# Top-2 expert routing rewritten: raw rows gathered, norms applied afterwards, choice per 128 tokens, overflow test moved into the first expert

## The reference

```
x = x + recurrent_mixer(rms_norm(x, norm_mix[1]), ...)
h = rms_norm(x, norm_ffn[1])
logits = h @ w_router                     # 8 experts
top_logits, top_idx = lax.top_k(logits, 2)
gates = softmax(top_logits)
# rows of h sorted by expert, in blocks of 128
y = (silu(xb @ w_gate[e]) * (xb @ w_up[e])) @ w_down[e]
x = x + sum over the token's two experts of gate * y
```

## Time and profile before

| | us |
|---|---|
| median of 3 runs | 2413.49 (2413.48 to 2413.81) |
| the profiled execution | 2411.67 |
| its span, first to last instruction | 2409.9 |
| PE busy | 2354.2 (98%) |
| DVE busy | 1801.3 (75%) |
| ACT busy | 1439.8 (60%) |
| chain that ended last | PE 88%, DVE 7%, ACT 2% |

### The profile page before, as it was taken

How to read it: one execution, slowest core, us unless ns; L and a number is a source line. 1 busy time by engine, 2 the same in 40 slices (tenths; PEclk the granted TensorE clock), 3 DMA queues, 4 the chain that set the end, 5 groups by cost and what they waited for, 6 DMA issues and landing times.

```text
span 2409.9 us, 30511 instructions
## 1 busy us (share of the span) xinstructions
PE 2354.2 (98%) x12200; PEld 1961.4 (81%) x12200; DVE 1801.3 (75%) x2391; ACT 1439.8 (60%) x1993; POOL 6.6 (0%) x15
## 2 busy tenths in 40 slices
PE   8999999799999999999999998999999999999998
PEld 7888888688888888888888886779988877898887
DVE  6755558798989898989898987676755577757554
ACT  5444446577777777777777775455444454545443
POOL 0000000000000000000000000000000000000000
PEclk9999999999999999999999999999999999999999
...
GB/s 277 122 192 184 184 181 161 186 343 361 349 357 359 366 338 357 358 371 345 351 358 360 360 334 165 168 121 179 171 189 182 175 187 122 140 176 167 194 185 58
DMA packets 277764, 586.40 MB, mean 243 GB/s; under 512 B 9216, under 2 KB 61568, under 8 KB 277616
## 3 DMA queue, kind: packets, MB, share of 16 engines
...
...
## 4 chain that ended last, share of the span: by engine, by line
PE 88%; DVE 7%; ACT 2%; issue 1%; DMA 0%; SPq 0%; DVEq 0%; ACTq 0%
PE ps L106 85%; PE ps L109 4%; DVE low_wlo L121 4%; ACT low_whi L115 1%; DMA low_raw<-in_hy_w_in 0%; ACT L112 0%; DVE low_nv L127 0%; ACT s_p L112 0%; ACT low_junk L112 0%; DVE s_rot L121 0%; DVE s_sm L121 0%; DVE s_G L121 0%; ACT rg_ra L112 0%; ACT s_zu L112 0%; DVE low_x L121 0%
## 5 line engine op out<-in xcount | busy, mean ns | idle before, releaser
L121 DVE TENSOR_TENSOR low_wlo<-low_raw,low_whi 128x1024 fp32r<-128x1024 f32 (+1 forms) x990 | 1159.3, 1214 | 364.0 <-ACT low_whi L115 362.9
L115 ACT CAST low_whi<-low_raw 128x1024 fp32r<-128x1024 f32 (+1 forms) x990 | 983.7, 1043 | 457.0 <-PE ps L106 444.4
L106 PE MATMUL ps<-low_whi,low_hTh 128*128 128x512 f32 (+2 forms) x1360 | 535.4, 394 | 7.3 <-DVE low_wlo L121 5.7
L106 PE MATMUL ps<-low_whi,low_hTl 128*128 128x512 f32 (+2 forms) x1360 | 521.3, 383 | 0.0
L106 PE MATMUL ps<-low_wlo,low_hTh 128*128 128x512 f32 (+2 forms) x1360 | 520.5, 383 | 0.0
L106 PEld LDWEIGHTS ps<-low_whi,low_hTh 128*128 128x128 f32 x1360 | 257.6, 189 | 55.1 <-DVE low_hTl L127 3.8
L106 PEld LDWEIGHTS ps<-low_whi,low_hTl 128*128 128x128 f32 x1360 | 256.9, 189 | 51.0
L106 PEld LDWEIGHTS ps<-low_wlo,low_hTh 128*128 128x128 f32 x1360 | 257.8, 190 | 44.5 <-issue 0.5
L106 PE MATMUL ps<-low_whi,ffn_Th 128*128 128x512 f32 x608 | 246.5, 405 | 0.0
L106 PE MATMUL ps<-low_wlo,ffn_Th 128*128 128x512 f32 x608 | 240.7, 396 | 0.0
L106 PE MATMUL ps<-low_whi,ffn_Tl 128*128 128x512 f32 x608 | 198.0, 396 | 0.0
...
## 6 DMA issues: line engine op xcount, KB each, us to landing
...
```

The costliest lines, as they stand in the source:

```text
L106: return self.real.matmul(*a, **k) if self.real else WALK
L115: return self.real.copy(*a) if self.real else WALK
L121: return self.real.tensor_tensor(*a) if self.real else WALK
```

## The change

1. The rows gathered are those of raw x: `hh` and `hl` are made from x, and `hf`, `grow` and its load go. The gain of the norm is applied to the gathered rows: `act_gather` and `dve_gather` work in two pieces of 128x256 with a scale per partition, for all pairs. The root is applied later: `pe_er` multiplies the one-hots with the root (one column per expert), `er` then scales the gate product in the silu and the up product in `f_h`. `pe_er` for experts 0 and 1 stands in step 0 before gate k-tile 5, for the other six in step 4 before up k-tile 5.
2. Choice, ranks, places and one-hots are made for each half of the tokens: `dve_choose`, `pe_ranks`, `dve_places`. The one-hots of half 0 are multiplied with the first 128 columns of a bank before those of half 1 exist (`pe_gather_first`).
3. The root is made once for both halves (`dve_rstd`), at the end of `dve_route`.
4. The shares are made in steps 2 to 4; the exp stands on ACT at the start of step 3. The table of silu is loaded at the end of `act_route`.
5. `where_over` stands before step 6 on PE, ACT and DVE, and on SP before the first load that waits for a unit after e0.u6.0. The piece that it skips uses other banks and other memory.
6. On ACT the cast of e0.g0.1 comes before `hh` of half 1, that of e0.u0.0 after the gather.

The diff, cut to its core (the removed lines stand above):

```diff
                     pe_router_x(e, 0, 0)
                 if (tb, n_half, n, q) == (1, 0, 1, 0):
                     pe_router_x(e, 0, 1)
+                if (tb, n_half, n, q) == (1, 0, 1, 1):
                     pe_router(e, 0, 0)
                 if (tb, n_half, n, q) == (1, 1, 0, 2):
                     pe_router(e, 0, 1)
...
+                t = e.matmul(AB[tb][:, 0:8], hT32[:, q, tb * 128:tb * 128 + 128], rw[:, q, :], start=q == 0, stop=q == 7)
+            if n:
+                t.then_inc(*mark("sum", "logits", tb))
...
+        def pe_gather_first(e, q, tb):
...
+            e.wait_ge(*at("hot", 1, tb))
+            e.wait_ge(*at("hl", tb, q // 2))
+            for i, t_ in ((0, 0),) if tb == 0 else ((0, 1), (1, 0), (1, 1)):
+                s, o = slice(128 * (2 * q + i), 128 * (2 * q + i) + 128), b[:, 256 * i:256 * i + 256]
+                e.matmul(o, hh[:, t_, s], S1[:, t_, 0:256], start=t_ == 0, stop=False)
+                t = e.matmul(o, hl[:, t_, s], S1[:, t_, 0:256], start=False, stop=t_ == 1)
+            if tb:
+                t.then_inc(*mark("gathered", 0, q))
...
+            for f in (2 * q, 2 * q + 1):
+                t = e.activation(xgs[p % 2][0][:, f, :], turns["gather", p, q][:, 256 * (f % 2):256 * (f % 2) + 256],
+                                 AF.Identity, scale=k("norm", 24 + f, 1))
+            t.then_inc(*mark("xh", p, q))
...
+            for f in (2 * q, 2 * q + 1):
+                t = e.scalar_tensor_tensor(xl[:, f, :], turns["gather", p, q][:, 256 * (f % 2):256 * (f % 2) + 256],
+                                           k("norm", 24 + f, 1), xh[:, f, :].bitcast(F32), MUL, SUB)
+            t.then_inc(*mark("xl", p, q))
...
+        def pe_er(e, x0, x1):
+            e.wait_ge(*at("rstd", "all"))
+            e.wait_ge(*at("hot", x1 - 1, 1))
+            for x_ in range(x0, x1):
+                for tb in range(2):
+                    t = e.matmul(b[:, x_:x_ + 1], S1[:, tb, 128 * x_:128 * x_ + 128].bitcast(F32), rs[:, 1, tb, 0:1],
+                                 start=tb == 0, stop=tb == 1)
+            t.then_inc(*mark("sum", "er", x0))
...
+        def pe_ranks(e, tb):
+            P = open_bank(e, 4, ("ranks", tb))
+            e.wait_ge(*at("chosen", tb))
+            t = e.matmul(P[:, 0:8], strict[:, :], Mb[:, tb, :], start=True, stop=tb == 0)
...
+            t.then_inc(*mark("sum", "ranks", tb))
         def pe_route(e):
             pe_router_x(e, 1, 0)
             pe_router_x(e, 1, 1)
+            pe_ranks(e, 0)
             pe_router(e, 1, 0)
+            pe_gather_first(e, 0, 0)
             pe_router(e, 1, 1)
...
+            for q in range(1, 4):
+                pe_gather_first(e, q, 0)
+            pe_ranks(e, 1)
             for q in range(4):
-                pe_gather(e, 0, q)
+                pe_gather_first(e, q, 1)
...
         def act_route(e):
+            for n in range(2):
+                act_hh(e, 0, n)
+                act_hT32(e, 0, n)
             act_sq(e, 3, 0, 0)
-            act_hT32(e, 0, 0)
             act_sq(e, 3, 0, 1)
-            act_hT32(e, 0, 1)
-            act_sq(e, 3, 1, 0)
-            act_hh(e, 0, 0)
-            act_hh(e, 0, 1)
+            hi_after(e, "rg.o.2")
+            act_hh(e, 1, 0)
             act_hT32(e, 1, 0)
             act_hT32(e, 1, 1)
+            act_hh(e, 1, 1)
+            act_sq(e, 3, 1, 0)
             act_sq(e, 3, 1, 1)
-            hi_after(e, "rg.o.2")
-            hi_after(e, "rg.o.3")
-            act_hh(e, 1, 0)
-            act_hh(e, 1, 1)
-            e.wait_ge(*at("share", 0))
-            e.activation(mexp, mdiff, AF.Exp).then_inc(*mark("share_e", "all"))
             for q in range(4):
                 act_gather(e, 0, q)
+            hi_after(e, "rg.o.3")
+            e.activation(msm[:, 254:255], msm[:, 255:256], AF.Silu)
...
+        def dve_rstd(e):
+            v, w, u = (nv[:, :, y] for y in range(3))
             for tb in range(2):
+                for n in range(2):
+                    e.wait_ge(*at("sq", 3, tb, n))
+            e.scalar_tensor_tensor(v, ss[:, :, 0], D * EPS, ss[:, :, 1], ADD, ADD).then_inc(*mark("step"))
+            rsqrt(e, v, w, u, False)
+            e.tensor_scalar(rs[:, 1, :, 0], w, -1 / 256, None, MUL).then_inc(*mark("rstd", "all"))
...
+        def dve_choose(e, tb):
+            e.wait_ge(*at("sum", "logits", tb))
...
+            e.tensor_tensor(meq[:, tb], mL[:, tb, :].unsqueeze(1).to_broadcast([128, 2, 8]),
+                            mtop[:, tb, 0:2].unsqueeze(2).to_broadcast([128, 2, 8]), EQ).then_inc(*mark("step"))
+            e.tensor_scalar(mnth[:, tb:tb + 1], mtop[:, tb, 0:1], mtop[:, tb, 1:2], 1.0, EQ, ADD).then_inc(*mark("step"))
+            e.wait_ge(sg.sem("step"), sg.count["step"] - 1)
+            e.tensor_tensor_scan(mcs[:, tb].rearrange("p k e -> p (k e)"), d0[:, :, :].rearrange("p k e -> p (k e)"),
+                                 meq[:, tb].rearrange("p k e -> p (k e)"), 0.0, MUL, ADD).then_inc(*mark("step"))
+            e.wait_ge(*now("step"))
...
+            e.tensor_tensor(Mb[:, tb, :], mmask[:, tb, 0], mmask[:, tb, 1], ADD).then_inc(*mark("chosen", tb))
...
+        def dve_places(e, tb):
+            n = 16 if tb else 8
+            e.wait_ge(*at("sum", "ranks", tb))
+            e.tensor_copy(posc[:, 8 * tb:8 * tb + n], AB[0][:, 0:n]).then_inc(*mark("ranks", tb))
+            e.wait_ge(*now("step"))
+            dve_hot(e, 0, tb)
+            dve_hot(e, 1, tb)
...
         def dve_route(e):
             dve_residual(e, 3, 0, 0)
             dve_residual(e, 3, 0, 1)
...
+            dve_hl(e, 0, 0)
+            dve_hl(e, 0, 1)
+            dve_choose(e, 0)
             dve_residual(e, 3, 1, 0)
...
             dve_residual(e, 3, 1, 1)
...
+            dve_places(e, 0)
+            dve_hl(e, 1, 0)
+            dve_choose(e, 1)
+            dve_hl(e, 1, 1)
+            dve_places(e, 1)
+            lo_after(e, "rg.o.2", 0)
+            dve_gather(e, 0, 0)
+            dve_gather(e, 0, 1)
+            lo_after(e, "rg.o.2")
+            dve_gather(e, 0, 2)
+            dve_gather(e, 0, 3)
+            lo_after(e, "rg.o.3")
+            dve_rstd(e)
+        def dve_share(e):
+            e.tensor_reduce(mmax, posc[:, 16:24], AX.X, MAX).then_inc(*mark("step"))
+            e.tensor_tensor(mdiff, mtop[:, :, 1], mtop[:, :, 0], SUB).then_inc(*mark("step"))
+            e.wait_ge(*at("rstd", "all"))
             e.wait_ge(*now("step"))
...
+            e.tensor_tensor(mdiff, rs[:, 1, :, 0], mdiff, MUL).then_inc(*mark("share", 0))
             e.tensor_copy(cnt[:, :], mmax).then_inc(*mark("count", "all"))
...
+        def act_share(e):
+            e.wait_ge(*at("share", 0))
+            e.activation(mexp, mdiff, AF.Exp).then_inc(*mark("share_e", "all"))
...
-            where_over(e, pe_overflow)
             for c_, (x_, f) in enumerate(STEPS):
+                if c_ == 6:
+                    where_over(e, pe_overflow)
                 for q in pe_gate_up(e, c_, "g", 0, "msilu"):
+                    if c_ == 0 and q == 5:
+                        pe_er(e, 0, 2)
                     if c_ == 1 and q == 2:
                         pe_expert_turn(e, 0)
...
                 for q in pe_gate_up(e, c_, "u", 1, "mprod"):
+                    if c_ == 4 and q == 5:
+                        pe_er(e, 2, EXPERTS)
...
         def act_moe(e):
             act_route(e)
-            where_over(e, act_overflow)
-            e.wait_ge(*at("moe", "all"))
-            e.activation(msm[:, 222:223], msm[:, 223:224], AF.Silu)
             for c_, (x_, f) in enumerate(STEPS):
                 tag = f"e{x_}"
+                if c_ == 3:
+                    act_share(e)
+                if c_ == 6:
+                    where_over(e, act_overflow)
                 if c_ == 1:
                     act_expert_T(e, 0)
                 hi_after(e, f"{tag}.g{f}.0")
...
                 e.wait_ge(*at("sum", "g", c_))
                 if c_ > 1:
                     e.wait_ge(*at("mprod", c_ - 2))
-                e.activation(f_g[:, c_ % 2, :], AB[0][:, :], AF.Silu).then_inc(*mark("msilu", c_))
+                e.wait_ge(*at("er", 0 if x_ < 2 else 2))
+                e.activation(f_g[:, c_ % 2, :], AB[0][:, :], AF.Silu, scale=er[:, x_:x_ + 1]).then_inc(*mark("msilu", c_))
...
             e.wait_ge(*at("msilu", c_))
             if c_ > 1:
                 e.wait_ge(*at("turned", "mh", c_ - 2))
-            e.tensor_tensor(f_h[:, y, :], f_g[:, y, :], AB[1][:, :], MUL).then_inc(*mark("mprod", c_))
+            x_ = STEPS[c_][0]
+            e.scalar_tensor_tensor(f_h[:, y, :], AB[1][:, :], er[:, x_:x_ + 1], f_g[:, y, :], MUL,
+                                   MUL).then_inc(*mark("mprod", c_))
...
         def dve_moe(e):
             dve_route(e)
-            where_over(e, dve_overflow)
-            e.memset(msm[:, 223:224], 0.0).then_inc(*mark("moe", "all"))
             for c_, (x_, f) in enumerate(STEPS):
                 tag = f"e{x_}"
```

(17 more changed lines are left out.)

208 lines of the change are left out of this document (81 added, 127 removed).

## The result

The changed kernel took 2418.77 us (median of 9 runs, 2415.71 to 2423.26) where the kernel before took 2411.54 us on the same chip (2410.80 to 2413.85): a ratio of 1.0028, interval 1.0017 to 1.0038. It is slower by 7 us where 2 us less was forecast, and outside the range given. The profiled execution has a span of 2416.4 us against 2409.9.

What follows compares the result with a forecast made beforehand. PE bounds the expert loop; the open time lies in the routing before the first product's transposes. -6.9 + 1.5 + 1.4 + 2.0 = -2.0 us gives span 2407.9, time 2411.5, range 2407.5 to 2415.5.

Steps and rivals of the forecast that it cites:

- Up to the second gather half: Routing before the gather of the second token half: that half starts at 448.9 instead of 454.75.
- The new wait: Step 0, before gate k-tile 5: PE stands 3 to 4.7 us for the root `rs`, ready at 460.0 or 461.0.
- From there to the mark: From `rs` to the first product's transposes: `pe_er` 0.5, k-tiles 2.1, up product 5.5, k-tiles 1.4; transposes at 469.5 or 470.5.
- -6.9: Gain at the first product's transposes, 476.92 before the change: 7.4 or 6.4 us, taken as -6.9.
- +1.5 for the clock: After PE's wait for `rs`, half clock doubles eleven or twelve 512-column matmuls: 0 to 2.7 us, taken as +1.5.
- Second `er`: Step 4 on PE: twelve more short matmuls at 0.12 each, +1.4 us.
- The branch: Overflow branch, now at step 6 in the full expert loop: +2.0 us, bounds 0 and 4.7.
- DVE lag: Step 6: after its branch DVE resumes at 568.95, product ends near 576.4; adds 0.7 to 1.7 us.
- PE's queue: At step 6, 16 to 20 queued matmuls last 3.7 to 4.6 us against 4.7 of load and branch; PE loses 0 to 1.
- Rival (c): Step 6: DVE's fetch under full DMA takes 9 us or more, deciding from about 8; sum +3 to +6, 2416.5 to 2419.5; chance 0.09.
- the rule of about 108 ns: Compare-and-branch at step 6 costs about 108 ns; by that alone the sum is -4.0, time 2409.5; chance 0.08.
- Rest: Exp and table load in step 3, share steps in 2 and 4, scaled products, `grow`'s load: all hidden or free, nothing added.

Runs made afterwards that it cites:

- the second: The changed kernel run once more, unaltered, for another trace: 2418.39 us (1 run) against 2413.37 for the kernel before.
- the one-pass form: The changed kernel with the `er` of experts 2 to 7 made by single two-column fp32r matmuls instead of fp32 ones: 2419.37 us, ratio 1.0026 to the kernel before.

## Why the prediction was wrong

- **Up to the second gather half: right.** 7.1 us after the x(1,0) transposes; forecast 448.9 - 442.4 = 6.5.
- **The new wait: right** in place, releaser and length (3 to 4.7 us; 4.04 measured). Its end came 19.1 us after the x(1,0) transposes, where the working had 17.6 to 18.6.
- **From there to the mark: mis-sized.** The `er` matmuls, priced at 0.5 like four router matmuls, took 1.86: each is two records, 0.12 at full and 0.23 at half clock, and they ran at half clock. That the sixteen rows of the router were eight matmuls is what I misread in the earlier trace rows. The forecast was -6.9 with +1.5 for the clock, -5.4; measured -2.93. That 2.5 is 1.4 on the `er` matmuls and some 1.0 by the later `rs`; the k-tiles at half clock (seven matmuls at an extra 0.2) used up the +1.5.
- **Second `er`: mis-sized by the same misreading.** 2.8 us instead of 1.4, confirmed by the one-pass form.
- **The branch: the step whose path was wrong.** The sum held +2.0, put together of a PE stop of 1 us and a DVE lag of 0.7 to 1.7; measured +4.23, all PE, in the first trace, and +2.65 in the second, of which 0.26 is DVE's. The fetch took 5.2 us instead of the 3.8 taken over from the old place. PE's queue was priced about right: from the register load on it covers 3.7 us (556.4 to 560.1), the low end of 3.7 to 4.6, but of 6.1 us and not of 4.7, so PE stood 2.4 and not 0 to 1. And half clock followed the stop (1.7), which I had charged to the `rs` wait alone. The DVE lag is there (DVE goes on at 568.67, forecast 568.95) but lies under PE's; that the product comes near 576.4 needs five more halves, as the order of the program has, not the four named. Rival (c) had a longer fetch, but on the wrong engine and with a threshold of 8 us that was not needed. That the full DMA makes the fetch longer fits all traces: 3.4 to 3.85 us in five jumps at a DMA share of 0 to 0.2, at two places, and 4.78 to 6.86 in seven at step 6 at a share near 1.0. No run changed the DMA share alone, and what moves it by 2 us between programs at the same share is open. Of the rule of about 108 ns (the Trainium skill, page "Advanced Engine Details and Errata", section "Control Flow Timing"): PE's jump over the code took 4.78 to 6.86 us, and 89 ns once it falls through; the figure fits the comparison alone, not a jump to code that has to be fetched.
- **What it cost before: not asked by itself.** The rows showed the branch stopping PE and DVE before step 0, and the -6.9 at the mark holds its going without a price. Without it the mark comes 1.2 us earlier, and the kernel before is no faster.
- **Rest:** put at nothing, the exp cost 0.3: its table load (1.28 us on ACT at 511.84) stands ahead of step 3's silu, and the product comes that much late (read from the trace, no run isolates it). Steps 7 to 55 lost 0.7, nearly all in pieces of 0.06 to 0.14, where the sum had nothing; their cause was not looked for.
- **The account.** With the true sizes (-2.93 + 0.29 + 2.78 + 4.23 + 0.66) the sum is +5.03 instead of -2.0. The 7.03 between them are 2.47 at the first product, 2.23 at the branch, 1.38 at the second `er` and 0.95 in the rest; the misread price of an fp32 matmul is 1.8 of them (0.9 more is the half clock on the first `er`). Another 2.66 behind the experts, less 1.19 of an earlier start, make the 6.5 between the spans; both are of the size by which traces of one kernel or of nearly equal ones differ there.
